# A two-layer transformer on one core: the output gates move from the attentions into the closing blocks

## The reference, cut to what matters

```
y = (o * silu(z)) @ w_out[i]                      # o: the attention's output, z: the gate, from x @ w_in
x = layernorm(alpha * x + y, ln_g[i], ln_b[i])
x = x + sigmoid(x @ pe_gate[i]) * (p[i] @ pe_proj[i])
```

## Time and profile before

| | us |
|---|---|
| median of 3 runs | 3240.16 |
| the profiled execution | 3234.05 |
| its span | 3232.2 |
| TensorE busy | 2960.0 (92%) |
| VectorE busy | 1913.8 (59%) |
| ScalarE busy | 1575.7 (49%) |
| GpSimd busy | 1244.5 (39%) |

### The profile page before, as it was taken

How to read it: one execution, slowest core, us unless ns; L and a number is a source line. 1 busy time by engine, 2 the same in 40 slices (tenths; PEclk the granted TensorE clock), 3 DMA queues, 4 the chain that set the end, 5 groups by cost and what they waited for, 6 DMA issues and landing times. The chain is left out here.

```text
span 3232.2 us, 40805 instructions
## 1 busy us (share of the span) xinstructions
PE 2960.0 (92%) x13514; PEld 2324.8 (72%) x13536; DVE 1913.8 (59%) x2771; ACT 1575.7 (49%) x2778; POOL 1244.5 (39%) x1044
## 2 busy tenths in 40 slices
PE   8999977778899999999677789999999999799998
PEld 6888875555688778888565467777777777578877
DVE  3544215444278774444555568778787787347875
ACT  3111114556444544444223167777777777544553
POOL 0022002223132541000210068888888888523353
PEclk9999988889899999999898789999999999899999
DMA  5255349664897665554567924252442522399764
GB/s 176 72 125 124 106 107 190 155 156 117 274 295 242 234 231 195 177 173 147 191 261 289 293 62 105 69 125 69 95 103 69 125 69 53 100 301 284 235 222 159
DMA packets 268849, 531.15 MB, mean 164 GB/s; under 512 B 46376, under 2 KB 94632, under 8 KB 260080
## 3 DMA queue, kind: packets, MB, share of 16 engines
q1 hardware_dynamic: 215696, 412.78, 44.5%
q10 hardware_dynamic: 52960, 116.02, 11.5%
HBM read 351.06 MB, written 177.37 MB: 163 GB/s over the span
## 5 line engine op out<-in xcount | busy, mean ns | idle before, releaser
L2161 POOL TENSOR_TENSOR mla_pl<-mla_p,mla_ph 128x512 fp32r<-128x512 f32 (+3 forms) x640 | 707.2, 1120 | 361.0 <-ACT mla_p L2023 352.5
L1324 PE MATMUL end_bank<-end_xh,end_whi 128*128 128x512 f32 x1600 | 633.1, 396 | 49.9 <-DVE end_xl L1510 28.7
L1325 PE MATMUL end_bank<-end_xl,end_whi 128*128 128x512 f32 x1600 | 625.0, 391 | 0.0
L1326 PE MATMUL end_bank<-end_xh,end_wlo 128*128 128x512 f32 x1600 | 625.0, 391 | 0.0
L1881 PE MATMUL mla_score<-mla_q,mla_k 96*128 96x512 f32 (+7 forms) x1920 | 555.7, 392 | 6.3 <-DMA mla_q<-mla_m_t 6.3
L1496 DVE TENSOR_TENSOR end_wlo<-end_wraw,end_whi 128x1024 fp32r<-128x1024 f32 x188 | 256.4, 1364 | 366.7 <-ACT end_whi L1379 366.2
L1379 ACT CAST end_whi<-end_wraw 128x1024 fp32r<-128x1024 f32 x188 | 197.2, 1049 | 552.8 <-PE end_bank L1326 516.2
L2022 ACT ACTIVATE mla_ph<-mla_score 128x512 fp32r<-128x512 f32 (+3 forms) x640 | 341.0, 533 | 225.8 <-PE mla_score L1881 222.8
L1881 PEld LDWEIGHTS mla_score<-mla_q,mla_k 96*128 96x128 f32 (+1 forms) x1920 | 362.8, 193 | 91.5 <-issue 36.8
L2053 DVE TENSOR_REDUCE mla_mx<-mla_mx 128x1 f32<-128x512 f32 (+3 forms) x640 | 371.9, 603 | 94.2 <-PE mla_mx L1881 93.6
L2099 DVE TENSOR_TENSOR mla_acc<-mla_acc,mla_p 128x512 f32<-128x512 f32 (+3 forms) x576 | 348.6, 605 | 118.6 <-ACT mla_p L2023 114.6
(11 more groups left out here) (233 smaller groups left out, 4695.7 us busy)
## 6 DMA issues: line engine op xcount, KB each, us to landing
end_wraw<-in_w_out ACTq DMA_DIRECT2D x64, 512.0 KB, 7.8
end_wraw<-in_pe_gate ACTq DMA_DIRECT2D x64, 512.0 KB, 4.8
end_wraw<-in_w_in ACTq DMA_DIRECT2D x56, 512.0 KB, 3.8
swa_q<-scratch_q_hi SPq DMA_DIRECT2D x32, 512.0 KB, 9.3
end_raw<-scratch_o SPq DMA_DIRECT2D x32, 512.0 KB, 11.7
end_factor<-scratch_inv SPq DMA_DIRECT2D x64, 256.0 KB, 10.0
scratch_proj<-end_out_f SPq DMA_DIRECT2D x64, 256.0 KB, 7.0
scratch_sum<-end_out_f SPq DMA_DIRECT2D x64, 256.0 KB, 6.5
```

The source lines that it names most:

```text
L1324: nc.tensor.matmul(bank, wh[:, at], xh[:, k0 + k, :], start=(k == 0), stop=False)
L1325: nc.tensor.matmul(bank, wh[:, at], xl[:, k0 + k, :], start=False, stop=False)
L1326: last = nc.tensor.matmul(bank, wl[:, at], xh[:, k0 + k, :], start=False, stop=(k == kc - 1))
L2161: pool.tensor_tensor(p_lo[b][:, off:TC], prob[b][:, off:TC], p_hi[b][:, off:TC].bitcast(F32), ALU.subtract).then_inc(p_lo_ok, 1)
```

## The change

Both attentions lose the gate: its load, its tiles, its multiplication, and the semaphore `gated`, whose waits go to `sum_ok`. In the local attention VectorE copies the bank to o_out; in the global one it writes its sum there. All low parts of the local attention go to GpSimd, masked steps and full ones alike. The closing block loads the gate, 128 x 1024 for every piece of a "wo" job, into the lo tile of the piece's set, and GpSimd multiplies once more, over the whole piece, behind the division. The factor's load waits for the division alone (`x_divided`).

```diff
@@ chain_phase
+        gate_in = [s.sem(f"gate_in{b}") for b in range(4)]
+        x_divided = s.sem("x_divided")
                     if f >= 2:
-                        sp.wait_ge(x_scaled, f - 1)
+                        sp.wait_ge(x_divided, f - 1)
+            def load_gate(n):
+                j, p = pieces[n]
+                wait_set_free(sp, j)
+                sp.dma_start(set_of(lo, n).bitcast(F32), cfg["gates"].rearrange("(k p) t -> p k t", p=P)[
+                    :, 2 * p:2 * p + 2, tok(jobs[j][1])]).then_inc(gate_in[p], 16)
                 if n >= 2:
                     store(n - 2)
+                for j, p in due(n, *load_parts):
+                    if jobs[j][0] == "wo":
+                        load_gate(piece_at[j, p])
@@ scale_x
-                op.then_inc(x_scaled, 1)
+                op.then_inc(x_divided, 1)
+                pool.wait_ge(x_divided, f + 1)
+                pool.wait_ge(gate_in[p], 16 * (f // 4 + 1))
+                pool.tensor_tensor(set_of(raw, n), set_of(raw, n), set_of(lo, n).bitcast(F32), ALU.mult
+                                   ).then_inc(x_scaled, 1)
@@ attention_phase
-            load_gate(0)
-                if c + 1 < len(chunks):
-                    load_gate(c + 1)
                     if not long:
-                        pe.wait_ge(gated, c - 1)
+                        pe.wait_ge(sum_ok, c - 1)
-                if on_vector(g):
-                    pe.wait_ge(p_lo_v_ok, low_count[g])
-                else:
-                    pe.wait_ge(p_lo_ok, low_count[g])
+                pe.wait_ge(p_lo_ok, g + 1)
-                act.wait_ge(gated, c + 1)
+                act.wait_ge(sum_ok, c + 1)
             def finish(c):
-                dve.wait_ge(low_ok, c + 1)
-                if c >= 2:
-                    dve.wait_ge(gated, c - 1)
-                vec.tensor_tensor(o_sum[c % 2][:], o_ps[c % 2][0:HEAD_DIM, :], o_low[c % 2][:], ALU.add
-                                  ).then_inc(sum_ok, 1)
                 if c >= small:
                     dve.wait_ge(stored[c % small], 16 * (c // small))
+                if not long:
+                    dve.wait_ge(weighed, last_of[c] + 1)
+                    vec.tensor_copy(o_out[c % small][:], o_ps[c % 2][0:HEAD_DIM, :]).then_inc(sum_ok, 1)
+                    return
+                dve.wait_ge(low_ok, c + 1)
+                vec.tensor_tensor(o_out[c % small][:], o_ps[c % 2][0:HEAD_DIM, :], o_low[c % 2][:], ALU.add
+                                  ).then_inc(sum_ok, 1)
@@ gpsimd of attention_phase
-            for g in range(total + tail):
-                if g < total and not on_vector(g):
+            for g in range(total):
                    ... the subtraction, for every step
-                if long and g - lag - 2 in closes:
-                    out_gate(closes[g - lag - 2])
```

More of the change, by code:

```diff
@@ L1752, in attention_phase @@
         mrow = [s.sem(f"max_row{b}") for b in range(2)]
[L1753 to L1758, removed]
+        stored, den_stored = ([s.sem(f"{n}{b}") for b in range(small)] for n in ("stored", "den_stored"))
+        (const_ok, scores, probs, p_lo_ok, acc_init, summed, weighed, mx_prod, mx_done, m_done, m_turned,
+         m_t_ok, low_ok, sum_ok, den_ok, row_ok) = (s.sem(n) for n in (
+             "const_ok", "scores", "probs", "p_lo_ok", "acc_init", "summed", "weighed", "mx_prod", "mx_done",
+             "m_done", "m_turned", "m_t_ok", "low_ok", "sum_ok", "den_ok", "row_ok"))
         block = ctx.enter_context(nc.Block())
@@ L1816, in at_slot @@
             return mine[k] if k < len(mine) and u + 1 < units else []
[L1818 to L1824, removed]
         tail = store_lag + 1
@@ L2007, in store @@
                               ).then_inc(den_stored[c % small], 16)
-                act.wait_ge(gated, c + 1)
-                act.dma_start(cfg["dst"](*chunks[c]), cfg["gate"](o_out[c % small])).then_inc(stored[c % small], 16)
+                act.wait_ge(sum_ok, c + 1)
+                act.dma_start(cfg["dst"](*chunks[c]), cfg["out"](o_out[c % small])).then_inc(stored[c % small], 16)
             max_row(0)
@@ L2129, in _ @@
                     u, k, st = flat[g]
-                    if on_vector(g):
-                        low_part(g)
                     for n in at_slot(u, k):
@@ L2139, in _ @@
                             negate(u + 1)
-                if not long and g - lag - 1 in closes:
-                    out_gate(closes[g - lag - 1])
-                if long and g - lag - 1 in closes:
+                if g - lag - 1 in closes:
                     finish(closes[g - lag - 1])
@@ L2231, in swa_config @@
                 mask_width=TC, load_a=load_a, load_b=load_b, n_load_a=8, n_load_b=6,
-                gate=lambda tile: tile[:].rearrange("d (j t) -> d j t", j=GROUP),
-                gate_src=lambda u, c: heads(gates, u, c), dst=lambda u, c: heads(out, u, c),
+                out=lambda tile: tile[:].rearrange("d (j t) -> d j t", j=GROUP),
+                dst=lambda u, c: heads(out, u, c),
                 q_view=lambda tile, c, off: tile.rearrange("r (j t) -> r j t", j=GROUP)[:, :, c * P:(c + 1) * P],
@@ L2239, in swa_config, with mla_config @@
                     u // 2, :, u % 2 * half_b:(u % 2 + 1) * half_b])
-def mla_config(q_nope, q_rope, k_nope, k_rope, v, gates, out, dens):
+def mla_config(q_nope, q_rope, k_nope, k_rope, v, out, dens):
     steps, items, gather = [], [], []
@@ L2283, in mla_config @@
                 load_a=load_a, load_b=load_b, n_load_a=5, n_load_b=6, gather=gather,
-                gate=lambda tile: tile[:], gate_src=lambda u, c: rows_of(gates, u, c),
+                out=lambda tile: tile[:],
                 dst=lambda u, c: rows_of(out, u, c),
@@ L2315, in spread, with close_layer @@
             return rows.rearrange("n (q c) -> (n q) c", c=cols)
-        def close_layer(layer, x, attn, sources, dst, latent=None):
+        def close_layer(layer, x, attn, gates, sources, dst, latent=None):
             inv = dram(f"inv{layer}", [HEADS, SEQ])
             chain_phase(nc, consts, f"end{layer}", dict(
-                o=attn, x=x, dst=dst, proj=dram(f"proj{layer}", [D_MODEL, SEQ]),
+                o=attn, gates=gates, x=x, dst=dst, proj=dram(f"proj{layer}", [D_MODEL, SEQ]),
                 summed=dram(f"sum{layer}", [D_MODEL, SEQ]), inv=inv, inv_spread=spread(inv),
```

46 lines of the change are left out of this document (11 added, 35 removed).

## The result

| | before | after |
|---|---|---|
| median, us | 3239.0 (5 runs, 3235.9 to 3241.09) | 3223.13 (5 runs, 3210.42 to 3224.26) |
| ratio, 95% interval | | 0.9943 (0.9924 to 0.9962) |
| the profiled execution, its span | 3234.05, 3232.2 | 3210.42, 3208.5 |

The kernel gained 16 us by the medians where 43 were forecast. The profiled execution of after is the lowest of its five.

What follows compares the result with a forecast made beforehand. TensorE, busy 92% of the span, was taken as the bound, its idle stretches winnable, one in the local attention behind late gates. -58 - 5 + 20 = -43 us gave 3191, or 3197 as a median; own range 3180 to 3220.

Steps and rivals of the forecast that it cites:

- Gates out of the local attention, -71: Local attention: without the gate stall five units fall from 42.4 to 28.2 us each, 71 us; first unit's 2.3 us wait goes too.
- Stores next, +12: Local attention: VectorE then waits for output stores, charged 2.5 us a unit, 12 us in all.
- Low parts on GpSimd, +2: Local attention: moving 60 subtractions from VectorE to GpSimd costs 2 us, with ends -2 and +10.
- the phase's sum, -58: Local attention: -71 - 2 + 12 + 2 + 1 = -58 us.
- startup: Local attention: 1 us charged for startup and tail beside the low parts' 2 us.
- Global attention, -5: Global attention: 64 multiplications leave GpSimd (82 us), gaining 0 to 9 us, taken as 5.
- Closing blocks, +20: Closing blocks: added gate loads cost DMA time, 28 us a layer, of which 10 a layer reach the time; ends -2 and 56.
- of the rest I let 4 through: Closing blocks: of the gate's other three quarters (21 us a layer), idle DMA time and buffers leave 4 us.
- VectorE is idle a fifth or more: Closing blocks: VectorE's idle fifth over 170 us absorbs its overlap with GpSimd's products, costing TensorE's path nothing.
- Rival C: Closing blocks bound by DMA: all 28 us a layer reach TensorE, its clock falls four times; +12, 3252 us; 12%.
- Rival A: Closing blocks hide the gates, nothing showing DMA engines can move over 303 GB/s against it; -63, 3177 us; 20%.
- rival B: Local attention: stores take the gates' place, units of 36.7 us, 30 us more in all; -13, 3227 us; 18%.

Runs made afterwards that it cites:

- e8: The change with six output tiles in place of three in the local attention: 3213.14 us, 0.9922 to the kernel before.
- e6: The kernel before with all low parts of the local attention on GpSimd and nothing else: 3229.61 us, ratio 0.9981.
- e10: The kernel before with local-attention gates loaded eight chunks ahead and all its low parts on GpSimd: 3189.63 us, ratio 0.9848.
- e11: The kernel before with local-attention gates eight chunks ahead, six output tiles and all low parts on GpSimd: 3180.42 us, ratio 0.9822.
- e9: The kernel before with gates eight chunks ahead and six output tiles in the local attention: 3181.43 us, ratio 0.9827.
- e7: The change in layer 0 alone, layer 1 as before (gate in the global attention, none in the last closing block): 3198.69 us, ratio 0.9873.
- e1: The changed kernel again, unaltered, for a second profile: 3217.61 us, 0.9931 to the kernel before; that profile's span is 3220.9 us.
- e2: The change without the gate in the closing blocks, neither loads nor products: 3178.41 us, 0.9813 to the kernel before.
- e3: The change with the gate loaded and waited for in the closing blocks but not multiplied: 3205.23 us, 0.9891 to the kernel before.
- e4: The change with no gate load in the closing blocks, the product kept, of the piece with itself: 3184.95 us, 0.9832 to the kernel before.
- e5: The kernel before with local-attention gates loaded eight chunks ahead, into ten tiles in place of three: 3197.05 us, ratio 0.9872.
- third batch: The last four experiments, timed on the first chip again; the kernel before had 3239.14 us there.

## Why the prediction was wrong

**Gates out of the local attention, -71:** right in mechanism, too large. No unit waits for a gate, and the clock is at 1.00. But the step took 28.2 us for a unit without a stall, from the one of before that had none. That unit was a lighter one: its window has 138 matmuls where the stalled ones have 155. With the stores' waits gone as well, a unit takes 30.3 us (e8), and TensorE is busy for 147.95 of the 151.4 us of five. So the five units gained 59.6 us (211.0 - 151.4) and not 71.

**Stores next, +12:** right in kind, twice too large. VectorE waited 26.9 us; e8 puts the price at 6.

**Low parts on GpSimd, +2:** wrong in sign. The step counted the engines' time and the slack in TensorE's order, and gave VectorE's relief at most 2 us. It is worth 3.9 to 7.5 us alone (e6) and 7 to 8 beside early gates (e10), but nothing measurable with six output tiles (e11 against e9).

So the phase's sum, -58 against -56.5, came out right by luck: the stall was over-valued by some 10 us (73 with the first unit's wait, against 62.7), and the stores (12 for 6) and the low parts with startup (3 for nothing or less) were overcharged by 9.

**Global attention, -5:** nothing measurable (e7: 974.5 against 973.7). GpSimd at 86% of that phase was not what TensorE waited for, as the waits said; the 5 were a guess inside 0 to 9.

**Closing blocks, +20: the step that failed.** The price is 39 us (e1 less e2), 34 to 46 in the two profiles. The mechanism, DMA time, was named, and its size at 28 us a layer. The first of its two terms held: of the quarter that falls into the projection the forecast passed 6 us on, and TensorE's waits for evictions grew by 6.2 us in the first profile (9.2 against 3.0) and by 5.1 in the second. The failing sentence is "of the rest I let 4 through". The first closing block grew by 17.3 and 24.1 us in the two profiles, so the rest let 11 and 19 through. Over both blocks, loads by themselves account for 13 us a layer (e3 less e2) and the product by itself for 3 (e4 less e2, not clear of noise). The forecast had fitted the product into idle time.

Why so much came through has two parts. One is my reading: a demand that lasts longer than the buffers' depth is not buffered, since they can lend their few tiles once. The other the trace shows, and the forecast missed it: it followed the late piece to TensorE (rounding, low part, 4 us left) and stopped there. TensorE hardly waited for that piece, 0.3 us at a time behind the first mark. It waited for weights, which stand behind the piece in ScalarE's order and, with a reciprocal of 3.35 us between, in VectorE's: 9.0 us in the second profile. The sentence that VectorE is idle a fifth or more there does not hold through its own rows either, which have it busy for 40.74 and 43.17 of 50 us.

Rival C had the right mechanism with every microsecond charged and a loss of clock four times on top. The clock did fall: to 0.50 from 810 to 815 in the first profile, and in the second to 0.66 from 927 to 932 and to 0.83 over 978 to 988. From these shares I estimate 1.7 us for each of the last two (5 x 0.34, 10 x 0.17), not C's 4.7. The sum stayed below its point of decision of 31 us a layer. Rival A is refuted by e2 (and the engines did move more than 303 GB/s, 337 in one window), rival B by units of 31.4 us where it had 36.7 (its own terms, four chunks at 6 us and four at 3, give 36).

The rule of the Trainium skill (SBUF — State Buffer, "SBUF: two separate sides") is that of a VectorE instruction with two SBUF inputs and a GpSimd one that reads SBUF the later waits for the whole of the other. The trace agrees: the three longest splits of the first profile, 3.0 us where one alone takes 1.2, started 0.4 to 0.5 us behind a product of 2.39 us (at 853.09 behind 852.65, at 898.32 behind 897.88, at 906.00 behind 905.54). That TensorE waits for splits by it was not shown; e4 puts the product with all it does at 6.5 us.

What is left open: why executions of the change spread from 3210 to 3224 us (those of the kernel before spread as far, 3232 to 3245 in the third batch). The two profiles put 11.5 of the 12.4 us between them into the closing blocks, and in the first one 5.2 of 6.9 us are the weights' low parts (3.8 against 9.0 us of waits), with a lower clock behind the longer stops. What makes the same chain come later in one execution than in another, no run tells.

## What to carry to other kernels

When work moves, price the place it moves to by its scarcest resource over the whole stretch. Here the DMA engines were near 1.0, and 28 us of added DMA time a layer cost 17 to 24 us, 13 of them by the loads alone; buffers did not hide it. Before moving a load because it comes late, look at what is queued ahead of it: issuing the same load earlier, into more tiles, took 40 us off with no work moved. And follow a late piece past its own consumer: on an engine that works in order the instructions behind it are late too, and here those, the weights, were what TensorE stopped for.

## What the hardware showed that I had not expected

- The same stop before the same instruction came with a fall of the clock in one execution and not in another: after 3.27 us the granted clock was 0.66 over the next 5 us (second profile), after 1.17 and 1.55 us it stayed at 1.00 (first profile).
- TensorE waited 17.9 us for outputs beside 25.5 us of VectorE's waits for stores in e5, and 10.6 beside 47.2 in e10: how long an engine waits says little of what it costs another.
- One GpSimd product of 128x1024 takes 2.39 us with two different inputs and 1.895 with the same input twice; two of 128x512 take 2.5.
- A DMA share of 1.02 beside a TensorE that never waits (e2) and one of 1.05 beside one that loses a tenth (e3: 41.49 of 46 us) look alike; the share alone did not tell how close to the edge the stretch was.
